# One stage for the sum of the experts, two norms and the second projection, in place of two stages

## The reference

```
x = x + g2 * _moe(h2_lat.reshape(-1, d), *moe_p).reshape(bsz, seq, d)
...
h = _rmsnorm(x, final_norm_g)                       # result of the first block
...
u = rms_norm(h, norm_g[l])                          # second block
proj = jnp.einsum('bsd,de->bse', u, w_in[l])
(q, k, v, z_att, f_raw, z_ssd, xbc, dt_raw, x_lru, z_lru) = jnp.split(proj, split_points, axis=-1)
...
h = h + jnp.einsum('bse,ed->bsd', mix, w_out[l])
```

## Time and profile before

| what | value |
|---|---|
| time, median of 3 runs | 4534.71 us (4532.52 to 4538.32) |
| time of the profiled execution | 4528.32 us |
| its span in the trace | 4526.6 us |
| PE busy | 3813.6 us (84%) |
| PEld busy | 2966.9 us (66%) |
| DVE busy | 2494.8 us (55%) |
| ACT busy | 1932.1 us (43%) |
| POOL busy | 880.0 us (19%) |
| mean granted TensorE clock | 0.923 |

### The profile page before, as it was taken

One profiled execution on the slowest core, in us unless ns is written; L12 is line 12 of the kernel. 1 busy time (PEld: TensorE's weight loads), 2 busy tenths in 40 slices (PEclk: granted clock), 3 DMA queues, 4 the chain that ended last, 5 costly groups with the idle time before them and its releaser, 6 DMA issues. The chain is left out here.

```text
span 4526.6 us, 91441 instructions
## 1 busy us (share of the span) xinstructions
PE 3813.6 (84%) x35497; PEld 2966.9 (66%) x35498; DVE 2494.8 (55%) x3876; ACT 1932.1 (43%) x2582; POOL 880.0 (19%) x812
## 2 busy tenths in 40 slices
PE   7599699677775877679999999999919989898679
PEld 1599689577675765256666666667617767766657
DVE  0388588555554656156656656666547655033731
ACT  0377476322221242056666666666622221044620
POOL 3100100133432001422222222222202233200000
PEclk9799799799898887889999999999959999999889
DMA  6444435322211542199899999544452222313442
GB/s 228 94 140 156 139 129 172 116 72 57 67 51 41 177 164 91 41 326 285 249 340 339 340 341 323 131 103 102 102 180 69 74 79 89 102 54 84 114 158 84
DMA packets 532079, 679.06 MB, mean 150 GB/s; under 512 B 75957, under 2 KB 422069, under 8 KB 531765
## 3 DMA queue, kind: packets, MB, share of 16 engines
q1 hardware_dynamic: 471880, 536.68, 36.4%
q0 software_dynamic: 39344, 135.94, 12.3%
q10 hardware_dynamic: 20544, 1.91, 0.4%
HBM read 500.48 MB, written 173.97 MB: 149 GB/s over the span
## 5 line engine op out<-in xcount | busy, mean ns | idle before, releaser
L2534 DVE TENSOR_TENSOR routed_w_low<-routed_wgu,routed_w_high 128x1024 fp32r<-128x1024 f32 x516 | 608.5, 1221 | 149.4 <-ACT routed_w_high L2483 142.1
L2483 ACT CAST routed_w_high<-routed_wgu 128x1024 fp32r x516 | 537.5, 1047 | 149.5 <-PE routed_p_gu L2457 89.0
L2439 PE MATMUL routed_p_y<-routed_wd,routed_hT 128*128 x1024 | 460.3, 592 | 1.7 <-ACT routed_y L2500 1.7
L2457 PE MATMUL routed_p_gu<-routed_w_high,routed_x_high 128*128 128x512 f32 x1024 | 417.3, 408 | 11.2 <-DVE routed_w_low L2534 11.2
L2457 PE MATMUL routed_p_gu<-routed_w_low,routed_x_high 128*128 128x512 f32 x1024 | 406.2, 397 | 0.0
L2457 PE MATMUL routed_p_gu<-routed_w_high,routed_x_low 128*128 128x512 f32 x1024 | 405.8, 396 | 0.0
L2402 POOL DMA_INDIRECT total<-routed_y,routed_yidx x128 | 202.7, 1583 | 906.0 <-ACT routed_y L2500 542.5
L511 PE MATMUL front_ps<-front_a_high,front_w_high 128*128 128x320 f32 (+1 forms) x1120 | 362.7, 324 | 16.5 <-DVE front_w_low L763 13.4
L511 PE MATMUL front_ps<-front_a_low,front_w_high 128*128 128x320 f32 (+1 forms) x1120 | 354.1, 316 | 0.0
L511 PE MATMUL front_ps<-front_a_high,front_w_low 128*128 128x320 f32 (+1 forms) x1120 | 353.9, 316 | 0.0
L2528 DVE TENSOR_TENSOR routed_x_low<-routed_p_x,routed_x_high 128x1024 fp32r<-128x1024 f32 x129 | 158.0, 1225 | 338.2 <-ACT routed_x_high L2478 335.6
(11 more groups left out here) (528 smaller groups left out, 7605.2 us busy)
## 6 DMA issues: line engine op xcount, KB each, us to landing
routed_wgu<-in_exp_w_gate_dram SPq DMA_DIRECT2D x64, 1024.0 KB
routed_wgu<-in_exp_w_up_dram SPq DMA_DIRECT2D x64, 1024.0 KB
routed_wd<-in_exp_w_down_dram SPq DMA_DIRECT2D x64, 1024.0 KB
front_wt<-in_w_in_dram SPq DMA_DIRECT2D x70, 512.0 KB, 4.3
mod_w<-in_w_mod_dram SPq DMA_DIRECT2D x12, 2048.0 KB
pre_wt<-in_w_in_dram SPq DMA_DIRECT2D x44, 512.0 KB, 3.9
out_a<-mix SPq DMA_DIRECT2D x24, 512.0 KB, 4.4
out_raw<-in_w_out_dram SPq DMA_DIRECT2D x24, 512.0 KB, 6.0
```

The lines of the kernel that those rows point to most:

```text
L2439: op = nc.tensor.matmul(p_y[:, h, :], hT[:, k, :], wd[:, bass.ds(e % WS, 1), k, h * BANK:(h + 1) * BANK], start=(k == 0), stop=(k == MT - 1))
L2457: op = nc.tensor.matmul(p_gu[:, :], x_part, w_part[:, k, :], start=(k == 0 and i == 0), stop=(k == KD - 1 and i == 2))
L2483: nc.scalar.copy(w_high[:, q * KQ:(q + 1) * KQ, :].rearrange("p k m -> p (k m)"), wgu[:, bass.ds(e % WS, 1), q * KQ:(q + 1) * KQ].rearrang ...
L2534: nc.vector.tensor_tensor(w_low[:, at, :].rearrange("p k m -> p (k m)"), wgu[:, bass.ds(e % WS, 1), at].rearrange("p o k j m -> p (o k j m)"),
```

## The change

`finish_first` and its stage `sum` are gone. `project_second` now gets `total`, the gain row, `x1` and both norms' weights, and its prelude does all of it: for a tile, x = x1 + total * gain; xg = x * last_g; two row sums, a of x squared and b of xg squared, both by ACT; then 1/sqrt(a + EPS) for h = xg times that, written by ACT and stored to `h` (which the end of the second block still reads), and, without going through h, 1/sqrt(EPS * (a + EPS) + b) for `yb`. `h` is not loaded again here. `total` is loaded into four buffers, `x1` into four others, the buffers being tiles which the loop uses later. A buffer for x1 is only loaded again when its store to `h` has landed (`h_sent`). All three weight rows are loaded from ACT's queue and DVE waits for all of them. The transposes write to `aux`, which leaves `ps` free: TensorE makes the first half of product 0 ahead of the transposes of tile 5 and the first half of product 1 ahead of those of tile 6, and leaves both out later. The parameters are issued in five parts: `params(0)`, 12 transfers, behind the first weights, and `params(1)` to `params(4)`, 8 transfers each, behind the store of tiles 1 to 4 and the loads of tiles 5 to 7.

```
         @block.sync  (project_second)
-            for t in range(LAT_TILES):
-                if t >= 2:
-                    sp.wait_ge(y_made, t - 1)
-                sp.dma_start(xb[:, t % 2, :], h[t * P:(t + 1) * P, :]).then_inc(x_ready[t % 2], 16)
-                if t == 1:
-                    weights(0)
-                    weights(1)
-                if t == 2:
...
+            def tile(t):
+                rows = slice(t * P, (t + 1) * P)
+                sp.dma_start(total_t[t % 4][:, :], total[rows, :]).then_inc(x_ready[t % 4], 16)
+                if t >= 4:
+                    sp.wait_ge(h_sent[t % 4], 16)
+                sp.dma_start(x_t[t % 4], x1[rows, :]).then_inc(x_ready[t % 4], 16)
...
+            for t in range(4):
+                tile(t)
+            weights(0)
+            weights(1)
+            params(0)
+            for t in range(LAT_TILES):
+                sp.wait_ge(h_made, t + 1)
+                sp.dma_start(h[t * P:(t + 1) * P, :], x_t[t % 4]).then_inc(h_sent[t % 4], 16)
+                if t + 4 < LAT_TILES:
+                    tile(t + 4)
+                if t >= 1:
+                    params(t)
...
         @block.tensor
+            def product(s, a, n):
+                u = s % 2
+                for k in range(KD):
+                    for j, (w_part, a_part) in enumerate(((w_high, a_high), (w_high, a_low), (w_low, a_high))):
+                        op = nc.tensor.matmul(ps[:, u, a:a + n], w_part[:, u, k, :], a_part[:, k, a:a + n],
+                                              start=(k == 0 and j == 0), stop=(k == KD - 1 and j == 2))
+                return op
+
             for t in range(LAT_TILES):
+                if t in (5, 6):
+                    pe.wait_ge(w_split, t - 4)
+                    pe.wait_ge(low_made, LAT_TILES // 2)
+                    product(t - 5, *parts[0])
                 pe.wait_ge(y_made, t + 1)
                 if t >= 2:
                     pe.wait_ge(low_made, t - 1)
...
                 pe.wait_ge(w_split, s + 1)
                 if s >= 2:
                     pe.wait_ge(evicted, s - 1)
...
+                    product(s, *parts[0])
+                product(s, *parts[1]).then_inc(mm_done, 1)
...
         @block.scalar
+            for j, row in enumerate((gain, last_g.rearrange("(o e) -> o e", o=1), norm_g.rearrange("(o e) -> o e", o=1))):
+                act.dma_start((gain_row, last_row, g_all)[j][:, :], row.broadcast_to([P, D])).then_inc(rows_loaded, 16)
             for t in range(LAT_TILES + 1):
                 if t < LAT_TILES:
                     u = t % 2
...
+                    act.wait_ge(x_made, t + 1)
+                    act.drain()
+                    nc.scalar.activation(xl[:, :], x_t[t % 4], ACT.Square, scale=D ** -0.5, accum_out=ms[:, u, 0:1])
+                    act.wait_ge(xg_made, t + 1)
+                    act.drain()
+                    nc.scalar.activation(xl[:, :], xv[:, u, :], ACT.Square, scale=D ** -0.5, accum_out=ms[:, u, 1:2]).then_inc(squared, 1)
                     act.wait_ge(mean, t + 1)
+                    nc.scalar.activation(ms[:, u, 2:4], ms[:, u, 2:4], ACT.Sqrt).then_inc(rooted, 1)
                 if t >= 1:
                     act.wait_ge(turned, t)
+                    nc.scalar.copy(a_high[:, :, (t - 1) * P:t * P], aux[:, (t - 1) % 2, :].rearrange("p (k t) -> p k t", k=KD))\
                         .then_inc(high_made, 1)
+                if t < LAT_TILES:
+                    act.wait_ge(inverted, t + 1)
+                    nc.scalar.activation(x_t[t % 4], xv[:, u, :], ACT.Copy, scale=ms[:, u, 4:5]).then_inc(h_made, 1)
...
         @block.vector
+            def gained(t):
+                dve.wait_ge(x_ready[t % 4], 32 * (t // 4 + 1))
+                nc.vector.tensor_tensor(total_t[t % 4][:, :], total_t[t % 4][:, :], gain_row[:, :], ALU.mult).then_inc(part_made, 1)
+
+            def low(t):
+                dve.wait_ge(high_made, t + 1)
+                nc.vector.tensor_tensor(a_low[:, :, t * P:(t + 1) * P], aux[:, t % 2, :].rearrange("p (k t) -> p k t", k=KD),
+                                        a_high[:, :, t * P:(t + 1) * P], ALU.subtract).then_inc(low_made, 1)
+
+            dve.wait_ge(rows_loaded, 48)
+            gained(0)
+            for t in range(LAT_TILES):
+                u = t % 2
+                dve.wait_ge(part_made, t + 1)
+                nc.vector.tensor_tensor(x_t[t % 4], x_t[t % 4], total_t[t % 4][:, :], ALU.add).then_inc(x_made, 1)
+                if t >= 2:
+                    dve.wait_ge(h_made, t - 1)
+                dve.wait_ge(x_made, t + 1)
+                nc.vector.tensor_tensor(xv[:, u, :], x_t[t % 4], last_row[:, :], ALU.mult).then_inc(xg_made, 1)
+                if t >= 2:
+                    low(t - 2)
+                dve.wait_ge(squared, t + 1)
+                nc.vector.tensor_scalar(ms[:, u, 2:3], ms[:, u, 0:1], EPS, None, ALU.add)
+                dve.drain()
+                nc.vector.scalar_tensor_tensor(ms[:, u, 3:4], ms[:, u, 2:3], EPS, ms[:, u, 1:2], ALU.mult, ALU.add).then_inc(mean, 1)
+                if t + 1 < LAT_TILES:
+                    gained(t + 1)
+                dve.wait_ge(rooted, t + 1)
+                nc.vector.reciprocal(ms[:, u, 4:6], ms[:, u, 2:4]).then_inc(inverted, 1)
+                dve.wait_ge(inverted, t + 1)
+                if t >= 2:
+                    dve.wait_ge(turned, t - 1)
+                nc.vector.scalar_tensor_tensor(yb[:, u, :], xv[:, u, :], ms[:, u, 5:6], g_all[:, :], ALU.mult, ALU.mult).then_inc(y_made, 1)
+            low(LAT_TILES - 2)
+            low(LAT_TILES - 1)
```

More of the change, by code:

```diff
@@ L3208, in _, with project_second @@
             finish(N // 2 - 1)
-def project_second(nc, consts, h, norm_g, w, par, proj, at, sd, mix):
+def project_second(nc, consts, total, gain, x1, last_g, h, norm_g, w, par, proj, at, sd, mix):
     order = [("small", 0, None)]
@@ L3243, in project_second @@
         g_all = st.sb("g_all", [P, D])
-        ms = st.sb("ms", [P, 2, 4])
+        ms = st.sb("ms", [P, 2, 6])
         gcol = st.sb("gcol", [P, 2])
@@ L3252, in project_second @@
         once, lam_loaded, zeroed = st.sem("once"), st.sem("lam_loaded"), st.sem("zeroed")
-        x_ready = [st.sem(f"x_ready{u}") for u in range(2)]
-        squared, mean, rooted, y_made, turned, high_made, low_made = (
-            st.sem(n) for n in ("squared", "mean", "rooted", "y_made", "turned", "high_made", "low_made"))
+        rows_loaded, part_made = st.sem("rows_loaded"), st.sem("part_made")
+        x_ready = [st.sem(f"x_ready{u}") for u in range(4)]
+        h_sent = [st.sem(f"h_sent{u}") for u in range(4)]
+        x_made, xg_made, squared, mean, rooted, inverted, h_made, y_made, turned, high_made, low_made = (
+            st.sem(n) for n in ("x_made", "xg_made", "squared", "mean", "rooted", "inverted", "h_made", "y_made", "turned", "high_made",
+                                "low_made"))
         w_ready = [st.sem(f"w_ready{u}") for u in range(2)]
@@ L3397, in _ @@
                     pe.wait_ge(evicted, s - 1)
-                for a, n in parts:
-                    for k in range(KD):
-                        for j, (w_part, a_part) in enumerate(((w_high, a_high), (w_high, a_low), (w_low, a_high))):
-                            op = nc.tensor.matmul(ps[:, u, a:a + n], w_part[:, u, k, :], a_part[:, k, a:a + n],
-                                                  start=(k == 0 and j == 0), stop=(k == KD - 1 and j == 2))
-                op.then_inc(mm_done, 1)
+                    product(s, *parts[0])
+                product(s, *parts[1]).then_inc(mm_done, 1)
                 m = qk_at_step(s, 1)
@@ L3445, in _ @@
             nc.scalar.activation(fcol[DT0:FT, 2:3], fcol[DT0:FT, 1:2], ACT.Exp)
+            for u in range(4):
+                act.wait_ge(h_sent[u], 16 * (LAT_TILES // 4))
             for s in range(N + 2):
@@ L3508, in _ @@
         def _(dve):
-            for t in range(LAT_TILES + 1):
-                if t < LAT_TILES:
-                    u = t % 2
-                    dve.wait_ge(squared, t + 1)
-                    nc.vector.tensor_scalar(ms[:, u, 1:2], ms[:, u, 0:1], 1.0 / D, EPS, ALU.mult, ALU.add).then_inc(mean, 1)
-                    dve.wait_ge(rooted, t + 1)
-                    nc.vector.reciprocal(ms[:, u, 3:4], ms[:, u, 2:3])
-                    dve.drain()
-                    if t == 0:
-                        dve.wait_ge(once, 16)
-                    else:
-                        dve.wait_ge(turned, t - 1)
-                    nc.vector.scalar_tensor_tensor(yb[:, u, :], xb[:, u, :], ms[:, u, 3:4], g_all[:, :], ALU.mult, ALU.mult)\
-                        .then_inc(y_made, 1)
-                if t >= 1:
-                    dve.wait_ge(high_made, t)
-                    high = a_high[:, :, (t - 1) * P:t * P]
-                    nc.vector.tensor_tensor(a_low[:, :, (t - 1) * P:t * P], ps[:, (t - 1) % 2, :].rearrange("p (k t) -> p k t", k=KD),
```

(4 more changed lines are left out.)

38 lines of the change are left out of this document (16 added, 22 removed).

## The result

The kernel after takes 4494.65 us (median of 4 runs, 4491.53 to 4501.17) and the kernel before 4533.61 (4530.7 to 4538.32) beside it: ratio 0.9912, 95% interval 0.9893 to 0.9931. It is 39 us faster; 33 were forecast, and 4502. The time lies inside the stated range of 4493 to 4512, 1.7 us from its fast end. The profiled execution took 4491.53 us, with a span of 4489.8.

A forecast was written before the change was run, and what follows sets the result against it. Bound: a 104.7 us passage where TensorE only transposes. Terms 12.9 + 48.3 + 11.8 + 5.0 + 5.5 = 83.5 against 118.3, 34.8 earlier; less 1.3 and 0.5, gain 33: 4502 us, range 4493 to 4512.

The forecast's parts named there:

- Case A: Main case for the merged prelude and what follows: DVE sets the pace; gain 27 to 39 us, chance 62%.
- a wait of TensorE of under 2 us at step 5: Sign that the forecast is wrong; it expected TensorE to wait 5 to 6 us there on step 3's eviction.
- case D: Rival at step 5: DVE's list does not hold it, TensorE keeps 5.5 us, no pause; gain 40, 4495, chance 8%.
- Start: Stage start: DVE waits 11.6 us for three broadcast rows, plus 1.3 for the first gain product: 12.9 us.
- A turn: One tile in the merged prelude: DVE nearly full, 6.9 us (bounds 6.65 and 9.0); seven turns 48.3.
- GpSimd: Splits of weights 0 and 1 beside full DVE turns in the prelude: cost 5 us, bounds 2 and 6.8.
- Last turn and halves: Prelude's end: last tile's turn and tail, delayed by TensorE's early half products; 11.8 us, bounds 10.2 to 16.
- Step 0: Its remaining 24 matmuls up to eviction, at the full clock after a 2.4 us pause: 5.5 us, else 7.8.
- After it: Behind step 0: half product becomes a 5.9 us pause, the clock falls; net cost 1.3, plus 0.5 for DVE's waits.
- SP, costed at nothing: SP's issuing in steps 1 to 4, 9.1 us against a 6.9 turn, covered by 9 us: no cost.
- case C: Rival: SP becomes the bound as stores land late and tile 7 comes late; gain 18 to 30, 4510, chance 10%.
- The wait for tile 3: Kernel before, prelude of `pre`: ScalarE stands 24.59 us because tile 3's load is issued behind the parameters.

The follow-up runs named there:

- e5: Kernel after, with a semaphore for each of the three broadcast rows, so VectorE waits for each only where it is used; 4470.1 us, one run.
- e4: Kernel after, with the loads of weights 0 and 1 moved behind tile 0's loads, ahead of tiles 1 to 3; 4461.5 us, ratio to kernel before 0.9907.
- e6: Kernel after, with GpSimd making the low part of weight tile 3 three times over, same result; 4467.1 us, one run.
- e9: Kernel after, unchanged, run and traced again; 4450.8 us, ratio to kernel before 0.9908.
- e3: Kernel after, with all five groups of parameters issued together behind the first weights; 4466.6 us, ratio to kernel before 0.9915.
- e1: Kernel after, without the two early half products: TensorE makes products 0 and 1 whole after the last tile; 4475.3 us, ratio to kernel before 0.9925.
- e2: Kernel before, both stages kept, with only the parameter transfers moved from behind tile 2's load to behind tile 7's; 4478.0 us, ratio to kernel before 0.9945.
- e7: Kernel after, with 16 more identity transposes by TensorE in its pause ahead of step 0's second half; 4462.3 us, one run.
- e8: Kernel after, with a semaphore for each broadcast row and the pause filled by 16 transposes; 4458.7 us, ratio to kernel before 0.9901.
- e10: e8 with the rows also issued in turn: second after the gain row landed, third after tile 0's loads; 4445.8 us, ratio to kernel before 0.9898.

## Why the prediction was right, and where its size was off

The time lies in the range. Case A came about up to step 0: VectorE set the pace, and no load held it. Behind step 0 it did not: one of the forecast's own signs of being wrong, a wait of TensorE of under 2 us at step 5, is there, with 1.65. The measured 4494.65 is the number of case D, but not its condition, since step 5 still waited for VectorE's list; the list was shorter, which no case had. That this fell inside the range is in part luck. Point by point:

*Start:* 12.9 us to the first sum, measured 13.0. The third row costs what the other two showed; e5 shows that 3.8 of it could be had back.

*A turn:* 6.9, measured 6.66; over seven turns 1.7 us better. The VectorE instructions stand nearly end to end, as the bound of 6.65 said.

*GpSimd:* 5.0, measured 4.5 (11.2 less 6.66), which is what three VectorE instructions lost beside it (0.83, 2.03 and 1.73). The rule of the Trainium skill, "SBUF — State Buffer", section "SBUF: two separate sides", speaks of whole instructions excluded; its 6.8 was too much here, because part of GpSimd's work lay in a wait of VectorE of 1.27 us. For single instructions it holds: 3.26 against 1.23.

*Last turn and halves:* 11.8, measured 9.5 (turn 7 began at 64.2, the first matmul came at 73.7). I costed transposes at the slow clock's 1.97 although the halves before them raise it; they took 1.04 and 1.09. That is 0.9 of the 2.3. The rest is that the clock rose after 7 matmuls of the first half and not 12, so that tile 6's transposes ended 4.9 us into turn 7 where I had 7.3, and nothing of the two halves reached the last turn.

*Step 0:* 5.5, measured 7.5. I took the clock to survive a pause of 2.4 us. Behind pauses of 2.74 to 2.80 us (e4, e6, e9) it was low at once and 13 or 14 of the 24 matmuls ran slow; behind 2.36 us it fell 1.1 and 1.3 us into the matmuls in the kernel after and e3, with 9 slow, and held in e5. The sum of the passage, 83.5, was measured as 81.2.

*After it:* this is the step that failed, in sign. I forecast a loss of 1.8 us: a pause of 5.9 at step 5, a fallen clock, and VectorE's waits. The pause was 1.65 and the clock stayed up, because VectorE's list took 41.0 and not 45.25. I had taken the list as fixed. It holds GpSimd's splits 2 to 5, the half product moved one of them from two VectorE instructions to under a reciprocal and another onto an instruction that lost less by it, and e1 (list back to 45.2) and e6 (45.6 with more splits) show that this is the cause. The same collision that I priced in the prelude I overlooked 40 us later. That e2 has the short list too, with neither the merge nor the halves, fits. The term was -1.8 and measured +4.2, with 0.8 more behind the list. Together 37.3 + 4.2 + 0.8 = 42.3 of way against 33; of the 9.3 us, 2.5 are the passage and 6.8 what lies behind it.

*SP, costed at nothing:* right, no wait on tiles 4 to 7; e3 shows the price beyond the cover, 10.2 us. Tile 7's x1 load, the last, was issued at 3347.00, landed 3.5 us later and was taken up at 3359.56, so case C was 9 us away.

*The wait for tile 3:* e2 shows that it goes without the merge: 19.8 us of passage, after 4.2 that the parameters then cost ahead of step 0. The 24.0 of its way hold 3.9 of the list's luck as well.

*Small slips in the sums:* the four GpSimd instructions in full make 6.74 and not 6.8, and the tail of the last tile before was 4.4, not 4.3. Neither moves the result.

The 0.8 us behind the list is a balance. TensorE's first wait for the recurrence's convolution is 3.2 us where it was 5.6 (5.6 in e2 too, 3.2 in all kernels with one stage), because three convolution products of VectorE, beside another of GpSimd's subtractions, took 4.6 us in place of 6.7: 2.4 gained. Behind that wait the stretch to TensorE's next one is 1.1 longer, with more of it at the low clock, and 0.7 is lost between the last such wait and attention's first load. That the three products are quicker by where the subtraction falls is likely, and no run tests it; the 0.7 is open, and so is what decides whether the clock falls behind waits of 2.4 to 3.2 us.

## What to carry to other kernels

Before merging stages to spare a trip through memory, look at what the loads stand behind in their queue: here one moved block of small transfers gave 24.0 us where the whole change gave 42.3. When an edit moves an instant, ask which unrelated pairs of VectorE and GpSimd instructions now meet or miss each other, up to the next point where VectorE is the chain; a fixed-looking list can change by a tenth (45.2 to 41.0 us). And wait for each constant where it is used, not for all of them at the first instruction.

## What the runs showed of the hardware

A GpSimd subtraction stretched not only VectorE instructions with two tile inputs (1.22 to 3.26 us) but also a TENSOR_SCALAR with one (0.69 to 2.72 us) and a SCALAR_TENSOR_TENSOR of 128x1 elements (0.16 to 1.89), while a RECIPROCAL of 6.54 us beside one whole subtraction and most of another kept its length. The subtraction itself took 2.34 us where it began first (at 3347.14 in the earlier trace rows) and 3.14 and 3.18 where it began inside a VectorE instruction (at 3316.21 in the kernel after, 3373.97 in e1).

TensorE's granted clock went to its lower level (1.2 GHz of 2.4) around an unfilled pause of 2.36 to 2.80 us ahead of step 0 in five traces of six: in three it was low when the pause ended, in two, of 2.36 us, it fell 1.1 and 1.3 us into the matmuls behind it. In the sixth, also of 2.36, it stayed up. In the three kernels whose pause held 1.9 us of transposes (e7, e8, e10) it stayed up. Of ten traces with the same 3.2 us wait of the loop it stayed up in two.

The broadcast of one row, issued behind 4 MB of loads on SP's queue, took about 7.2 us to land.
